# Head by head first quarter, loads of two query blocks into the ring, and a state-space loop mixed with top-k

## The chip, the cores and the metric

The program runs on one core of a Trainium2 chip. A core has a matrix engine (PE, with its weight loads as PEld), a vector engine (DVE), a scalar engine (ACT), a general engine (POOL, which here only issues gathers once the start is over), a queue engine (SP, which issues the plain loads) and 16 DMA engines that all loads share. The metric is the device time of one execution in microseconds, a median over runs.

## What is computed

A decoder trunk of two layers over 256 positions of width 1024, in float32. Layer 0 mixes with a state-space layer (64 groups of 16 channels, 64 complex states each, then a gated projection, GLU), layer 1 with dilated attention. Each is followed by a PEER channel mixer, which is where most of the time goes. Cut to what matters:

```python
def s5_mixer(h, ...):                  # per group: s[t] = a * s[t-1] + B u[t]; y = Re(C s) + d * h
    ...
    y = jax.nn.gelu(y).astype(h.dtype)
    z = y @ w_glu
    val, gate = jnp.split(z, 2, axis=-1)
    return val * jax.nn.sigmoid(gate)

def peer_ffn(h, w_q, sub_keys, u_tab, v_tab):
    q = (h @ w_q).reshape(bsz, seq, PEER_HEADS, 2, PEER_HALF)       # 8 heads, 2 halves of 128
    s = jnp.einsum('blhpe,hpne->blhpn', q, sub_keys)                # 128 keys a half
    s_top, i_top = lax.top_k(s, PEER_TOPK)                          # 16 of 128, each half
    cand = s_top[..., 0, :, None] + s_top[..., 1, None, :]          # 256 sums a head
    best, pos = lax.top_k(cand, PEER_TOPK)                          # 16 experts a head
    gate = jax.nn.softmax(best, axis=-1)
    # per token: sum over 8 * 16 experts of gate * gelu(u_e . h) * v_e
```

Every token reads 128 rows of u and v (8 KB an expert), chosen by its own top-k.

## The kernel before

The 256 positions are two chunks of 128, so there are four **phases**: PEER of layer 0 for chunk 0 (phase 0) and chunk 1, then of layer 1 for both. A phase is 128 gathers ("slots"). One gather (L1160, POOL) is an indirect DMA of 128 rows, 1.05 MB, into one of eight ring places in `ringmem`. DVE multiplies the u part with the spread activations and sums it (L1189, "a dot product"), ACT applies gelu and the gate (L773, L777, L782), PE multiplies the v part into PSUM (L419). Slots go in **pairs** (64 a phase). Gather s waits until PE has used pair (s - 8) // 2 (`v_pe`), so POOL runs at most eight slots ahead.

While phase p runs, the engines also do the next dense stage: in phase 0 it is layer 0 for chunk 1. Every engine has one instruction stream, written by hand, and `g.at(phase, n)` puts in the slots of the first n pairs before what follows. So `g.at` points set the whole order: in phase 0 the state-space loop starts at pair 14 with a step every 4 pairs (`S5_AT, S5_K = 14, 4`), the GLU projections stand at 46 to 49, the norm at 51, the next PEER scores from 54.

Eight heads go in four **quarters** of two heads. A quarter is 32 of the 128 slots. For each: PE projects queries from one 2.1 MB block of w_q (L492, 32 matmuls, which the trace shows as 64 records), ACT copies them (`copy_q`, L966), PE scores them against the keys (`score`, L588), DVE does the top-k in four parts (`best_of_halves`, `sum_pairs`, `best_of_sums`, `find_experts`, L1426 to L1488), and ACT lays the indices out as gather rows (`gate_quarter`, L850 to L859), which counts up `idx_ready`. Only then can the gathers of that quarter go. In phase 0 the first quarter runs before any gather. DVE then has the parts of quarters 1 to 3 at points 1 to 12 (`other_quarters(0, 1)`), each behind one more pair, and the state-space loop follows. A step k of that loop is PE's input product (`s5_bu`, L529), DVE's rotation (`s5_rotate`, L1293 to L1301) and scan (`s5_scan`, L1311 to L1319), PE's output product (`s5_y`, L548) and ACT's gelu. There are eight steps (KT = 8).

All quarters of the top-k share one scratch place (`qs` and gT). Weights go through two places, `wt[:, 0]` and `wt[:, 1]`, in one numbered sequence of items (`weights`): item n is loaded when item n - 2 is used. SP issues them in the order of its stream, so one that waits holds up all behind it.

## Time and profile before

| | |
|---|---|
| median of 3 runs | 1776.49 us (1765.98 to 1777.57) |
| profiled execution | 1767.9 us, span 1766.1 us, granted TensorE clock 0.858 |
| busy, share of span | PE 72%, DVE 63%, ACT 38%, POOL 35% |
| DMA | 685.81 MB, mean 388 GB/s; gathers 536.90 MB |
| chain that ended last | PE 34%, DMA 32%, DVE 18%, ACT 8%, issue 5%, POOL 3% |

The page cuts the span into 40 slices of 44 us; the rows of the section below come from it and from answers about single stretches. Times in a timeline are from the start of the span. "Idle before <- X" says what ended an engine's wait. The share of DMA is the mean busy share of its 16 engines; values a little over 1 are full.

### The profile page before, as it was taken

To read this page: it belongs to the slowest core of one execution; us is meant where nothing else is said; L and a number is where in the kernel's file an instruction comes from. 1 tells how busy PE (TensorE), PEld (TensorE's weight loads), DVE (VectorE), ACT (ScalarE), POOL (GpSimd) and SP (SyncE) were. 2 spreads that over 40 slices of the span, in tenths; PEclk is the share of its full clock that TensorE was granted. 3 is DMA by queue.
4 is the path that set the end of the run, shared out by engine and by line. 5 is a ranking of instruction groups with operands and counts; after the bars stand their busy time and mean duration, and the time that the engine had idled before them with its cause. 6 is when DMAs were issued, how large, how long until landed. Compare 5 with 4: busy or idle time off the path is not lost.

```text
span 1766.1 us, 17527 instructions
## 1 busy us (share of the span) xinstructions
PE 1279.0 (72%) x5714; PEld 537.8 (30%) x5714; DVE 1118.9 (63%) x2512; ACT 675.6 (38%) x2012; POOL 616.9 (35%) x557
## 2 busy tenths in 40 slices
PE   3884455576976988997778599799886965555554
PEld 2471011122721333333345133443352720000000
DVE  8859888973569656435346975553553577666554
ACT  7634522222243338217323432741572243233222
POOL 4213243442243224324322322332432254444341
PEclk9998667789987988999898799899998987676777
DMA  8059999999998999999999899999999989999996
GB/s 330 7 232 380 380 420 397 410 413 423 423 421 338 425 424 421 423 425 421 423 424 416 342 416 424 421 357 426 422 372 424 404 356 416 416 417 410 421 421 291
DMA packets 86636, 685.81 MB, mean 388 GB/s; under 512 B 9872, under 2 KB 10256, under 8 KB 12176
## 3 DMA queue, kind: packets, MB, share of 16 engines
q0 software_dynamic: 73728, 536.90, 74.2%
q1 hardware_dynamic: 12816, 147.79, 20.0%
q8 instruction: 45, 0.74, 0.2%
q14 instruction: 47, 0.39, 0.1%
HBM read 683.60 MB, written 1.05 MB: 388 GB/s over the span
## 4 chain that ended last, share of the span: by engine, by line
PE 34%; DMA 32%; DVE 18%; ACT 8%; issue 5%; POOL 3%; SPq 0%; POOLq 0%; ACTq 0%; DVEq 0%
DMA ringmem<-experts,lay 22%; PE ps L480 12%; PE ps L419 11%; DMA wt<-w_qkv 7%; PE ps L492 6%; DVE ringmem L1189 5%; POOL ringmem L1160 3%; DMA wt<-w_o 2%; ACT lay L850 2%; ACT S L782 2%; PE ps L432 1%; PE ps L661 1%; ACT L777 1%; PE ps L686 1%; DMA wt<-w_glu 1%
## 5 line engine op out<-in xcount | busy, mean ns | idle before, releaser
L1160 POOL DMA_INDIRECT ringmem<-experts,lay x512 | 585.4, 1143 | 1070.9 <-PE ps L419 939.6
L419 PE MATMUL ps<-ringmem,S 128*32 128x512 f32 x2048 | 619.6, 765 | 389.0 <-ACT S L782 387.0
L1189 DVE CUSTOM_DVE_ANT_0 ringmem<-ringmem,Hrep 128x1024 f32<-128x1024 f32 x384 | 460.7, 1223 | 256.1 <-DMA ringmem<-experts,lay 251.3
L419 PEld LDWEIGHTS ps<-ringmem,S 128*32 128x32 f32 x2048 | 113.8, 126 | 800.2 <-ACT S L782 547.4
L777 ACT ACTIVATE gelus<-dots 128x2 f32<-128x2 f32 x256 | 51.6, 202 | 593.5 <-DVE dots L1189 592.5
L480 PE MATMUL ps<-wt,hT 128*128 128x512 f32 x576 | 256.2, 598 | 13.8 <-DMA wt<-w_qkv 13.8
L1189 DVE CUSTOM_DVE_ANT_0 ringmem<-ringmem,area 128x1024 f32<-128x1024 f32 x128 | 155.7, 1224 | 119.4 <-DMA ringmem<-experts,lay 118.4
L480 PEld LDWEIGHTS ps<-wt,hT 128*128 128x128 f32 x576 | 106.5, 190 | 164.0 <-issue 158.7
L773 ACT ACTIVATE S<-con,lay 128x32 f32<-128x32 f32 x512 | 134.6, 311 | 50.7 <-PE ps L419 50.0
L782 ACT ACTIVATE S<-S,gelus 128x32 f32<-128x32 f32 x512 | 136.7, 314 | 24.8 <-ACT gelus L777 1.5
L492 PEld LDWEIGHTS ps<-hT,wt 128*128 128x128 f32 x1024 | 117.4, 194 | 10.6 <-issue 10.3
L492 PE MATMUL ps<-hT,wt 128*128 128x128 f32 x1024 | 120.1, 279 | 0.0
L480 PE MATMUL ps<-wt,gT 128*128 128x512 f32 x128 | 62.3, 643 | 12.4 <-DMA wt<-w_o 10.5
L777 ACT ACT_TABLE_LOAD x55 | 70.6, 1283 | 1.0
L850 ACT COPY lay<-sel 32x16 f32<-32x16 f32 x256 | 51.5, 201 | 38.4 <-DVE sel L1488 35.6
L1509 DVE TENSOR_TENSOR area<-ps,con 128x512 f32<-128x512 f32 x24 | 16.6, 691 | 75.3 <-PE ps L480 63.1
L1024 ACT COPY area<-ps 128x512 f32<-128x512 f32 x12 | 7.0, 586 | 141.4 <-PE ps L480 141.4
L1524 DVE CUSTOM_DVE_ANT_0 area<-ps,area 128x384 f32<-128x384 f32 (+1 forms) x32 | 24.2, 757 | 46.1 <-PE ps L661 46.1
L1426 DVE MAX8 qs<-ps 128x8 f32<-128x128 f32 x64 | 14.2, 283 | 53.9 <-PE ps L515 42.7
L661 PE MATMUL ps<-area 64*128 64x128 f32 x288 | 43.2, 295 | 0.0
L1189 DVE DVE_READ_ACCUMULATOR2_ANT dots<- 128x1 f32 x512 | 41.7, 81 | 0.0
L998 ACT ACT_TABLE_LOAD x32 | 41.1, 1283 | 0.6
(201 smaller groups left out, 1163.4 us busy)
## 6 DMA issues: line engine op xcount, KB each, us to landing
wt<-w_qkv SPq DMA_DIRECT2D x36, 2048.0 KB, 11.6
wt<-w_q SPq DMA_DIRECT2D x16, 2048.0 KB, 11.4
wt<-w_glu SPq DMA_DIRECT2D x5, 2048.0 KB, 12.6
ringmem<-experts,lay POOLq DMA_INDIRECT x512, 12.5
wt<-w_o SPq DMA_DIRECT2D x4, 2048.0 KB, 14.5
ringmem<-w_glu SPq DMA_DIRECT2D x3, 2048.0 KB, 21.4
gain<-gains SPq DMA_DIRECT2D x9, 512.0 KB, 14.4
area<-keys SPq DMA_DIRECT2D x4, 1024.0 KB, 9.6
```

The costliest lines, as they stand in the source:

```text
L419: last = pe.matmul(ps[TG * t:TG * (t + 1), half, :], S[:, u % 2, i, :], ring[:, (2 * u + i) % RING, D + half * 512:D + (half + 1) * 512], ...
L480: last = pe.matmul(ps[:, bank, :], act[:, k, :], wt[:, n % 2, k, :], start=(k == 0), stop=(k == KT - 1))
L492: last = pe.matmul(ps[:, bank, m * P:(m + 1) * P], wt[:, n % 2, k, m * P:(m + 1) * P], hT[:, k, :], start=(k == 0 and m == 0), stop=(k == ...
L661: last = pe.matmul(ps[:, 2 + at // 512, at % 512:at % 512 + P], QT[rows, gr, h // 2, :], kt, start=True, stop=True, skip_group_check=True)
L773: last = act.activation(S[:, u % 2, i, :], own, ACT.Copy, scale=lay[:, phase % NC, 1, j - 1 + i, n:n + 1])
L777: act.activation(gelus[:, u % 2, :], dots[:, u % 2, :], ACT.Gelu_apprx_tanh).then_inc(gelu_ready, 1)
L782: last = act.activation(S[:, u % 2, i, :], S[:, u % 2, i, :], ACT.Copy, scale=gelus[:, u % 2, i:i + 1])
L850: last = act.copy(lay[TG * r:TG * (r + 1), ph % NC, :, j, n:n + QPQ], sel[TG * j:TG * (j + 1), :, QPQ * r:QPQ * (r + 1)])
L998: act.activation(SS[u % 2][:, 0:n], SS[u % 2][:, 0:n], ACT.Exp, bias=nmx[:, u:u + 1], scale=DH ** -0.5, accum_out=den[:, u:u + 1]).then_in ...
L1160: pool.indirect_dma_start(ring[:, s % RING, :], None, experts[phase // NC], bass.IndirectOffsetOnAxis(ap=rows[:, phase % NC, j, n:n + 1], ...
L1189: last = v.tensor_tensor_reduce(ring[:, i, 0:D], ring[:, i, 0:D], hrep(phase, j), 1.0, 0.0, ALU.mult, ALU.add, dots[:, b, second:second + 1])
L1524: v.tensor_tensor_reduce(SS[u % 2][:, 0:n], banks(2, 4)[:, at:at + n], mask[:, 0:n], 1.0, NEG, ALU.add, ALU.max, mx[:, u:u + 1]).then_inc( ...
```

## The change

Phase 0 and the dense stage beside it are put in another order; arithmetic and bytes stay the same.

- **First quarter head by head.** PE projects head 0 alone (parts 0 and 1), scores it, and DVE and ACT take its top-k and rows to the end; then head 1. `idx_ready` counts one more, and POOL waits for the second head at slot 16.
- **w_q blocks of quarters 2 and 3 in the ring.** They are loaded into ring places 4 to 7 as soon as the GLU weights there are used, and projected before quarter 1. Gathers 4 and 6 wait for these projections (`wq_used`). Quarters 2, 3 and 1 are all scored before DVE begins quarter 1.
- **Own places for the top-k of quarters 2 and 3,** in `wt[:, 1]`, to which ACT copies their scores. So `wt[:, 1]` holds no weights until their rows are done: only the first GLU block of chunk 1 is loaded early.
- **State-space loop mixed with top-k.** Quarter 1's parts stand at points 4 to 7, those of quarters 2 and 3 at 9 to 34, and the loop's steps at 10 to 46, first step four pairs earlier, the end at 46 as before.

The diff, cut to its core (the top-k functions take their tiles from `top_k_at` and run over the heads they are given, else as before):

```diff
--- before.py
+++ after.py
...
+WT0 = 2
...
+    if layer == 0:
+        return i - WQ0 if c == 0 else WT0 + i
+    return WT0 + ITEMS0 + ITEMS1 * c + i
...
+        wq_ring = [view(ringmem, 4096 * i, KT, BLOCK) for i in (2, 3)]
...
+        late = wt[:, 1].rearrange("p k n -> p (k n)")
+        late_scores = [view(late, 1024 + 512 * i, QHP, NKEYS) for i in range(2)]
+        places = top_k_places(qs, gflat)
+        late_places = top_k_places(late[:, 2048:2560], late)
+
+        def top_k_at(ph, i):
+
+            return late_places if ph == 0 and i >= 2 else places
+
...
+        def event(ph, i, heads=(0, QH)):
+
+            if ph == 0 and i == 0:
+                return heads[1]
+            return QUARTERS * ph + i + 2
+
+        FIRST = [(0, 0, (h, h + 1)) for h in range(QH)]
+        BANKS0 = (5, 6, 7, 4)
+        PARTS0_AT = (4, 5, 6, 7, 9, 13, 17, 21, 25, 27, 30, 34)
...
+        S5_AT = 10, 14, 19, 23, 28, 32, 37, 41, 46
...
-        S5_AT, S5_K = 14, 4
...
-            weights(0, 0, 6, 8)
             next_gain(2, 0)
-            sp.wait_ge(idx_ready, QUARTERS)
-            weights(0, 1, 0, 2)
+            sp.wait_ge(glu_used, 4)
+            for i in range(2):
+                sp.dma_start(wq_ring[i].rearrange("p k n -> p (k n)"), w_q[0, 2 + i]).then_inc(wq_in[i], 16)
+            weights(0, 1, 0, 1)
             next_gain(3, 1)
-            weights(0, 1, 2, 6)
+            sp.wait_ge(idx_ready, event(0, QUARTERS - 1))
+            weights(0, 1, 1, 6)
             load_keys(1, glu_done, 2)
...
-                project_turned(item(0, 0, WQ0), 4, e)
+                project_turned(item(0, 0, WQ0), 4, e, parts=(0, 1), done=first_q)
                 pe.wait_ge(keys_in, 16)
-                score(0)
+                score(1, 4, 0, (0, 1))
                 pe.wait_ge(con_in, 16)
                 spread_first()
-                for i in range(1, QUARTERS + 1):
-                    if i < QUARTERS:
-                        project_turned(item(0, 0, WQ0 + i), 4 + i)
-                    if i >= 2:
-                        score(i - 1)
+                project_turned(item(0, 0, WQ0), BANKS0[0], parts=(2, 3))
+                score(2, BANKS0[0], 0, (2, 3))
+                pe.wait_ge(best_ready, 1)
+                for i in (2, 3):
+                    pe.wait_ge(wq_in[i - 2], 16)
+                    project_turned(None, BANKS0[i], done=wq_used, w=wq_ring[i - 2])
+                g.at(0, 1)
+                score(3, BANKS0[2], 2)
+                score(4, BANKS0[3], 3)
+                g.at(0, 2)
+                project_turned(item(0, 0, WQ0 + 1), BANKS0[1])
+                g.at(0, 3)
+                score(5, BANKS0[1], 1)
 
...
-                    g.at(gphase, S5_AT)
+                    g.at(gphase, S5_AT[0])
                     pe.wait_ge(hT_ready, e + 1)
-                    pe.wait_ge(idx_ready, QUARTERS)
+                    pe.wait_ge(best_ready, event(0, 1))
+                    pe.wait_ge(score_copied, 1)
...
-                copy_q(0)
+                def copy_q(i, bank, parts=slice(0, QHP)):
+                    act.copy(qT[:, i % 2, parts].rearrange("p k t -> p (k t)"),
+                             ps[:, bank, P * parts.start:P * parts.stop]).then_inc(q_copied, 1)
+
+                act.wait_ge(first_q, 1)
+                copy_q(0, 4, slice(0, 2))
                 act.wait_ge(z0_ready, KT)
                 spread_h()
-                gate_quarter(0, 0)
-                for i in range(1, QUARTERS):
-                    copy_q(i)
+                gate_quarter(*FIRST[0])
+                act.wait_ge(w_used, item(0, 0, WQ0) + 1)
+                copy_q(0, BANKS0[0], slice(2, 4))
+                gate_quarter(*FIRST[1])
+                act.wait_ge(wq_used, 1)
+                act.wait_ge(score_done, 2)
+                copy_q(2, BANKS0[2])
+                g.at(0, 1)
+                act.wait_ge(wq_used, 2)
+                copy_q(3, BANKS0[3])
+                g.at(0, 3)
+                act.wait_ge(w_used, item(0, 0, WQ0 + 1) + 1)
+                act.wait_ge(score_done, 4)
+                copy_q(1, BANKS0[1])
+                for i in range(2):
+                    last = act.copy(late_scores[i].rearrange("p a n -> p (a n)"), ps[:, BANKS0[2 + i], :])
+                last.then_inc(score_copied, 1)
+                g.at(0, PARTS0_AT[0])
+                copy_turn(hT, turned, norm_event(0, 1, 0) + 1, hT_ready)
+                g.at(0, PARTS0_AT[3])
+                gate_quarter(0, 1)
 
...
-                copy_turn(hT, turned, e + 1, hT_ready)
...
+                for n in range(S5_AT[0] + 1, S5_AT[KT] + 1):
+                    g.at(gphase, n)
+                    if n in PARTS0_AT[7::4]:
+                        gate_quarter(0, PARTS0_AT.index(n) // TOPK_PARTS + 1)
+                    if n in S5_AT:
+                        k = S5_AT.index(n) - 1
+                        if k + 1 < KT:
+                            spread_step(k + 1)
+                        gelu_y(c, k)
                 g.at(gphase, GLU_AT + 4)
...
+                if phase == 0 and at == QSTEPS // QH:
+                    pool.wait_ge(idx_ready, event(0, 0))
+                if s in (4, 6):
+                    pool.wait_ge(wq_used, s // 2 - 1)
...
-                top_k(None, 0, 0, 0)
+                top_k(None, 0, *FIRST[0])
 
             def layer0(gphase, c):
-                for k in range(KT):
-                    if k == 0:
-                        g.at(gphase, S5_AT + 1)
+                for n in range(PARTS0_AT[0], S5_AT[KT] + 1):
+                    g.at(gphase, n)
+                    if n in PARTS0_AT:
+                        i, part = divmod(PARTS0_AT.index(n), TOPK_PARTS)
+                        top_k_part(0, i + 1, part)
+                    if n == S5_AT[0]:
                         v.wait_ge(z0_ready, KT)
                         v.tensor_tensor(z0re, z0re, mag, ALU.mult)
                         link(v.tensor_tensor(z0im, z0im, mag, ALU.mult))
+                    if n == S5_AT[0] + 2:
+                        s5_scan(c, 0)
+                    if n - 1 in S5_AT[1:KT]:
+                        s5_scan(c, S5_AT.index(n - 1))
+                    if n == S5_AT[0] + 1:
                         s5_rotate(c, 0)
-                    g.at(gphase, S5_AT + S5_K * k + 1)
-                    s5_scan(c, k)
-                    g.at(gphase, S5_AT + S5_K * (k + 1))
-                    if k + 1 < KT:
-                        s5_rotate(c, k + 1)
+                    if n in S5_AT[1:KT]:
+                        s5_rotate(c, S5_AT.index(n))
...
+                w = top_k_at(ph, i)
+                if ph == 0 and i >= 2:
+                    sc = late_scores[i - 2]
+                    v.wait_ge(score_copied, 1)
+                else:
+                    bank = 4 + i if ph else 4 if heads == (0, 1) else BANKS0[i]
+                    sc = ps[:, bank, :].rearrange("p (a n) -> p a n", a=QHP)
...
-            other_quarters(0, 1)
+            top_k(None, 0, *FIRST[1])
```

PE between the first PEER projection and the state-space loop, before. L492 is a projection, L588 a score group, L432 the spread of the activations, L458 the transpose for chunk 1, L419 the slots (4 matmuls a pair).

```order
L470 MATMUL ps<-con,H 128x128 x8
L492 MATMUL ps<-hT,wt 128x128 x32
L588 MATMUL ps<-area 128x128 x4
L432 MATMUL ps<-H,con 128x512 x8
L492 MATMUL ps<-hT,wt 128x128 x64
L588 MATMUL ps<-area 128x128 x4
L492 MATMUL ps<-hT,wt 128x128 x32
L588 MATMUL ps<-area 128x128 x8
L458 MATMUL ps<-con,H 128x128 x8
L419 MATMUL ps<-ringmem,S 32x512 x56
```

The same place on PE in the change, where L523 is a projection, L619 a score group, L461 the spread and L448 the slots.

```order
L523 MATMUL ps<-hT,wt 128x128 x16
L619 MATMUL ps<-area 128x128 x2
L461 MATMUL ps<-H,con 128x512 x8
L523 MATMUL ps<-hT,wt 128x128 x16
L619 MATMUL ps<-area 128x128 x2
L523 MATMUL ps<-hT,ringmem 128x128 x64
L448 MATMUL ps<-ringmem,S 32x512 x4
L619 MATMUL ps<-area 128x128 x8
L448 MATMUL ps<-ringmem,S 32x512 x4
L523 MATMUL ps<-hT,wt 128x128 x32
L448 MATMUL ps<-ringmem,S 32x512 x4
L619 MATMUL ps<-area 128x128 x4
```

The first projection and score group are halved, quarters 2 and 3 go first, and three pairs now stand ahead of the scores of quarter 1.

DVE between the scan of step 2 and the rotation of step 3 of the loop, before. L1317 to L1319 end the scan, L1189 is a dot product and the read of its sum (three pairs stand here, one dot product is shown), L1293 begins the rotation.

```order
L1317 TENSOR_TENSOR area<-area 128x512
L1318 SCALAR_TENSOR_TENSOR area<-area 128x512
L1319 TENSOR_TENSOR area<-area 128x512
L1189 ISA ringmem,dots<-ringmem,Hrep 128x1024
L1189 ISA dots 128x1
L1293 TENSOR_TENSOR area<-area,ps 128x512
```

The same place in the change: one pair, then the last part of a top-k in `wt`, then two pairs and the rotation (L1361).

```order
L1387 TENSOR_TENSOR area<-area 128x512
L1257 ISA ringmem,dots<-ringmem,Hrep 128x1024
L1257 ISA dots 128x1
L1558 TENSOR_SCALAR wt<-wt 128x32
L1559 TENSOR_SCALAR wt<-wt 128x32
L1561 CAST wt<-wt 128x64
L1566 TENSOR_TENSOR wt<-wt,con 128x1024
L1570 TENSOR_TENSOR wt<-wt 128x512 x2
L1573 TENSOR_REDUCE wt<-wt 128x64
L1576 SCALAR_TENSOR_TENSOR sel<-wt 128x32
L1581 TENSOR_TENSOR sel<-wt 128x32
L1361 TENSOR_TENSOR area<-area,ps 128x512
```

A part of top-k has moved into the space between two steps of the loop, on the same engine.

## Rows read from the trace of the kernel before

**Rows 1.** The page: the span, and what the DMA engines moved in 40 slices.

```profile
span 1766.1 us, 17527 instructions
...
GB/s 330 7 232 380 380 420 397 410 413 423 423 421 338 425 424 421 423 425 421 423 424 416 342 416 424 421 357 426 422 372 424 404 356 416 416 417 410 421 421 291
```

**Rows 2.** Stretches: us, busy PE, PEld, DVE, ACT, POOL, granted clock, DMA share, GB/s.

```profile
94.50:122.70 28.20, 27.43 (x196) 24.10 (x196) 15.17 (x64) 8.22 (x20) 0.00 (x0) 0.93 0.38 141
...
134.90:211.00 76.10, 34.04 (x118) 8.14 (x116) 74.45 (x239) 34.98 (x125) 26.56 (x24) 0.73 0.92 372
211.00:246.00 35.00, 17.34 (x113) 4.93 (x113) 26.03 (x47) 10.48 (x40) 13.19 (x12) 0.70 1.01 423
246.00:383.40 137.40, 81.20 (x525) 22.51 (x526) 122.07 (x198) 38.67 (x152) 57.38 (x52) 0.72 1.00 408
```

**Rows 3.** Timeline from first PEER projection to first gather: start, us, engine, line.

```profile
94.51 9.34 PE L492 MATMUL ps<-hT,wt 128*128 128x128 f32 x64
...
103.88 0.59 ACT L966 COPY area<-ps 128x512 f32<-128x512 f32 x1 [8.47 <-PE ps L492]
...
105.84 0.89 DVE L1426 MAX8 qs<-ps 128x8 f32<-128x128 f32 x4 [11.19 <-PE ps L588]
...
110.72 14.56 PE L492 MATMUL ps<-hT,wt 128*128 128x128 f32 x128
...
121.15 0.19 DVE L1488 TENSOR_TENSOR sel<-qs 128x32 f32<-128x32 f32 x1
...
121.37 0.84 ACT L850 COPY lay<-sel 32x16 f32<-32x16 f32 x4 [5.68 <-DVE sel L1488]
...
122.73 1.12 POOL L1160 DMA_INDIRECT ringmem<-experts,lay  x1 [39.13 <-ACT lay L854]
```

**Rows 4.** Timeline of DVE over one quarter's top-k with four pairs between.

```profile
159.50 0.89 DVE L1426 MAX8 qs<-ps 128x8 f32<-128x128 f32 x4
...
162.68 1.23 DVE L1189 CUSTOM_DVE_ANT_0 ringmem<-ringmem,Hrep 128x1024 f32<-128x1024 f32 x1
...
164.97 0.87 DVE L1435 MAX8 qs<-gT 128x8 f32<-128x128 f32 x4
...
184.08 0.89 DVE L1426 MAX8 qs<-ps 128x8 f32<-128x128 f32 x4
```

**Rows 5.** Timeline of one step of the state-space loop, and a pair's way to its gather.

```profile
260.06 0.69 DVE L1293 TENSOR_TENSOR area<-area,ps 128x512 f32<-128x512 f32 x1 [1.01 <-issue]
...
264.49 1.23 DVE L1189 CUSTOM_DVE_ANT_0 ringmem<-ringmem,Hrep 128x1024 f32<-128x1024 f32 x1
...
266.79 1.22 DVE L1311 TENSOR_TENSOR_SCAN area<-qs,area 128x512 f32<-128x512 f32 x1
...
267.79 3.63 PE L419 MATMUL ps<-ringmem,S 128*32 128x512 f32 x8 [5.12 <-ACT S L782]
...
271.70 0.94 POOL L1160 DMA_INDIRECT ringmem<-experts,lay  x1 [6.57 <-PE ps L419]
271.72 1.24 DVE L1189 CUSTOM_DVE_ANT_0 ringmem<-ringmem,Hrep 128x1024 f32<-128x1024 f32 x1
```

**Rows 6.** Waits of DVE, 134.9 to 383.4 us: total, times, longest.

```profile
DVE ringmem L1189 <- DMA ringmem<-experts,lay: 10.4, 11, 2.1
DVE area L1293 <- issue: 8.5, 6, 2.1
DVE area L1293 <- PE ps L529: 3.6, 1, 3.6
```

**Rows 7.** A stretch in the columns of rows 2.

```profile
95.00:100.00 5.00, 5.00 (x32) 5.00 (x32) 0.00 (x0) 0.41 (x2) 0.00 (x0) 0.64 0.19 77
```

**Rows 8.** Gathers to 389 us and their way to landing; DVE at dot product 91.

```profile
L1160 POOL DMA_INDIRECT ringmem<-experts,lay x100: 932/938/1974, 122.7 to 388.3; - x100
...
DMA to landing us min/median/max: 5.6/10.6/21.8
...
382.13 1.26 DVE L1189 CUSTOM_DVE_ANT_0 ringmem<-ringmem,Hrep 128x1024 f32<-128x1024 f32 x1 [1.14 <-DMA ringmem<-experts,lay]
```

More of the change, by code:

```diff
@@ L21 @@
+from collections import namedtuple
 from contextlib import ExitStack
@@ L227, in build @@
         glu_used = sem("glu_used")
+        wq_in = [sem(f"wq_in{i}") for i in range(2)]
+        wq_used = sem("wq_used")
         w_used = sem("w_used")
@@ L263, in build @@
         q_copied = sem("q_copied")
+        first_q = sem("first_q")
         score_done = sem("score_done")
@@ L1448, in best_of_sums @@
-            def best_of_sums(ph, c, i):
-                cand2 = S2.rearrange("p (h two) n -> p h (two n)", two=2)
-                for h in range(QH):
-                    last = v.max(best[:, h, 0:8], cand[:, h, :])
+                hs = slice(*heads)
+                ms = slice(2 * heads[0], 2 * heads[1])
+                pairs = w.stop.rearrange("p (h two) k -> p h two k", two=2)
+                v.tensor_copy(w.itopf[:, ms], w.itop[:, ms])
+                shape = [P, heads[1] - heads[0], TOPK, TOPK]
@@ new lines, in sum_pairs, with best_of_sums @@
+                link(v.tensor_tensor(w.cand.rearrange("p h (i j) -> p h i j", j=TOPK)[:, hs],
+                                     spread(pairs[:, hs, 0, :], 3, shape),
+                                     spread(pairs[:, hs, 1, :], 2, shape), ALU.add))
+            def best_of_sums(ph, i, heads):
+                w = top_k_at(ph, i)
+                cand2 = w.S2.rearrange("p (h two) n -> p h (two n)", two=2)
+                hs = slice(*heads)
+                for h in range(*heads):
+                    last = v.max(w.best[:, h, 0:8], w.cand[:, h, :])
```

219 lines of the change are left out of this document (107 added, 112 removed).

## The prediction

> **What bounds the kernel now.** I read the slices of the page first: of the 40 slices of 44 us, the second and third move 7 and 232 GB/s, the fourth and fifth 380, and nearly all behind them close to 420 [rows 1]. The 512 gathers of 1.05 MB are 537 of 686 MB, so past the first gather time is bytes over rate plus DMA idle. The table by stretch [rows 2] shows where DMA is idle: from 94.5 us (first PEER projection) to the first gather it is busy 0.38 of 28.2 us, 17.5 us idle, and from 134.9 to 211.0 us it is busy 0.92 of 76.1 us, 6.1 us idle. Those 23.6 us are all that an earlier start and a better mix can win in phase 0. The same table says who holds DMA back in the second stretch: DVE is busy 74.45 of 76.10 us (top-k of quarters 1 to 3). In the state-space loop it is busy 122.07 of 137.40 us, with DMA just full at 408 GB/s. So in phase 0 **two** limits lie close together: DMA, 2.48 us a gather at 423 GB/s (2.57 at the loop's 408), and DVE. After phase 0 nothing is touched: the reworked top-k helpers issue the same instructions on the same number of elements there.
>
> **DVE's prices, start to start.** A dot product takes 1.15 us, a pair 2.30 (162.68 to 164.97). One quarter's top-k and four pairs take 184.08 - 159.50 = 24.58 us, so the top-k is 24.58 - 9.20 = 15.4 us; its first part is 162.68 - 159.50 = 3.2 [rows 4]. A state-space step is a rotation of 264.49 - 260.06 = 4.43 and a scan of 271.72 - 266.79 = 4.93, together 9.36 us [rows 5].
>
> **First gather.** The projection of head 0 is 32 of the 64 records of 9.34 us; the stretch 95 to 100 us holds 32 records, so it ends near 99.7, 4.2 us before [rows 3, 7]. Copy and scores halve: -0.7. Of the 15.4 us of top-k some ten instructions are as small as the last one (0.19 us, some 0.14 start to start) and keep their time, 1.4 us; the rest halves: 1.4 + 7.0 = 8.4, so -7.0. First gather: 122.73 - 11.9 = 110.8 us [rows 3]. This is the gain the change makes. The two w_q blocks (4.2 MB, 10 us at 423 GB/s) and a gain load now run from 95 to 106, where DMA was idle.
>
> **What it costs behind.** ACT copies head 1's queries only after head 0's index rows: those ended 4.4 us after 121.3, so now 109.4 + 4.4 = 113.8, and PE gets them at 114.2, scores done at 115.0. PE has by then sat 5 us. It then has quarters 2 and 3 (14.6 us at full clock, the 128 records of 14.56 [rows 3]), pair 0, two score groups, pair 1, quarter 1 (7.3), pair 2, and the score group of quarter 1, which is the one DVE needs next. With 2.6 us for a pair (between 3.63 at half clock [rows 5] and half of it) and 1.1 for a score group: 115.0 + 14.6 + 2.0 (a start at half clock, as 9.34 - 7.28 of the first projection) + 2.6 + 2.2 + 2.6 + 7.3 + 2.6 + 1.1 = 150.0 us. Gathers 4 to 7 also wait for the ring slots that hold w_q, to about 124 and 131.6. DVE has head 1 (8.4 us from 115) and pairs 0 to 3 done by 140 and then waits 10 us. So **quarter 1's top-k starts at 150 with four pairs done, where before it started at 134.9 with one**: three pairs are worth 6.9 us, the delay is 15.1, and DVE is 8 us behind. Bounds: 148 with every projection at full clock; 157 with quarter 1's projection wholly at half.
>
> Two edits I cost at nothing: the copies of the late scores (two of the kind of 0.59 [rows 3]) run on ACT while DVE waits for quarter 1, and ACT is busy 34.98 of 76.10 us [rows 2]; and the late top-k reads and writes SBUF places instead of PSUM and gT, on as many elements. If a late part cost 10% more, DVE would lose 3 us.
>
> **The mixed stretch.** From pair 9 to pair 34 DVE now has 25 pairs (57.5), two top-k (30.8) and six steps (56.2): 144.5 us, 5.8 a pair, before any wait, where DMA needs 4.95 to 5.14. Both regimes that are alternated load DVE, so DVE stays the bound. Its waits: before, 8.5 + 3.6 us over seven of the eight rotations on PE, up to 2.1 each, 3.6 for the first [rows 6]. Now rotations 1 and 4 stand behind a top-k part and wait for nothing; 2 and 5 pay 2.1, and 3 waits for pairs that ACT holds up behind a gate quarter (3.4 us of copies), say 3.0. With the first's 3.6 that is 10.8, and I add 2.1 for small ones: 12.9 us to point 34 (5 to 17). Pair 33 ends at 150.0 + 30 x 2.30 + 46.2 + 56.2 + 0.2 + 12.9 less the last part of 5.0 behind it = 329.5. From a pair's last dot product to its gather takes 271.70 - 266.87 = 4.8 us [rows 5], the second of two 1.2 more, and landing at least 5.6 [rows 8]: gather 75 lands at 341.1. Before, gather 91 had landed at 382.1 and 16 gathers at 2.57 are 41.1: gather 75 at 341.0 [rows 8]. Equal, but before had read both first w_glu blocks of chunk 1 by then and the new order has one of them left: 2.1 MB, 5.0 us. A further 1.8 us of DMA idle I put beside the gate of the last quarter at point 34. Gather 91 then lands at 341.1 + 5.0 + 41.1 + 1.8 = 389.0, **6.9 us later than before** at the same bytes. The same from DVE alone: 150.0 + 42 x 2.30 + 46.2 + 74.9 + 0.2 + 19.2 (the 12.9, 4.2 for rotation 6 behind the last gate, 2.1 for rotation 7) = 387.1 against 383.3 now, +3.8; the later of the two counts. Behind it everything is DMA-bound in both. The sum: 12 us won at the first gather, given back between 110 and 340 with 7 us on top. The profiled execution (span 1766.1, 1767.9 with what lies around it) becomes 1774.8; the median of the three runs is 1776.49, so I forecast 1783.4 in its terms. This case's own range: waits 5 to 17 and start 148 to 157 give -4 to +18.
>
> The Trainium skill, Perfetto Trace Analysis, section Optimization Strategy, says performance may improve by interleaving regimes whose most-contended engine differs. That would favour this change; rows 2 show DVE as the fullest engine in both regimes, so its condition isn't met here.
>
> **Rivals.** (a) *The early start survives.* If quarter 1 is scored by 140 and the ring of eight (four pairs, 20 us of gathers) bridges DVE's lag, DMA never starves: gain 12 us, at most 23.6 less the 6 us between the w_q loads and the first gather, 17.6: 1759 to 1765. For it: DVE idles 10.4 us on DMA before, which it could use. Against it: 5.8 us a pair over 25 pairs is a lag of 17 to 21 us without waits. (b) *PE's clock.* PE sat idle before the first projection and the granted clock was 0.64 in 95 to 100 us [rows 7]; the new order puts 5 us of idle before quarters 2 and 3 and small gaps before quarter 1. If all three run at 1.2 instead of 2.4 GHz, quarter 1's scores come up to 3 x 7.3 - 2 = 20 us later; with quarter 1 and half of the others 11 to 13: the kernel ends 18 to 25 us later, 1795 to 1808. It decides from about 10 us of extra PE time. The Trainium skill, TensorE: Matmul & The Clock Gate, Part 1, says the throttled clock is the default and activity lifts it; the trace agrees (0.64 there with 9.34 us for 64 records, then 14.56 us for 128 [rows 3]). (c) *Nothing shows.* DVE's lag and the won start cancel within 4 us, 1773 to 1781.
>
> **Chances.** Forecast 0.50; (a) 0.18, of which 0.11 beyond 1%; (b) 0.20, nearly all beyond 1%; (c) 0.12. One per cent is 17.8 us, about what a measurement of this kernel can tell from no change. Faster 0.12, same 0.66, slower 0.22 ((b) and the top of the forecast). The range 1762 to 1804 leaves out 0.1 of (a) below and less than 0.1 of (b) above.
>
> **What would show it.** First gather at 110 to 112 us; gathers 4 and 6 waiting on PE to about 124 and 131; DVE idle some 10 us before quarter 1's first MAX8, which starts near 150; DVE over 0.93 busy and DMA under 400 GB/s between 165 and 330 us; rotation waits near zero for the second and fifth; gather 99 issued about 7 us later than 388.3. It is wrong if quarter 1 starts before 145, or if DMA moves 420 GB/s through the mixed stretch: then (a).

## The result, and the profile after

| | before | the change |
|---|---|---|
| median | 1773.01 us (1764.5 to 1777.57, 10 runs) | 1784.22 us (1775.89 to 1795.96, 10 runs) |
| ratio, 95% interval | | 1.0073 (1.0047 to 1.010) |
| profiled execution, span | 1766.1 us | 1782.1 us |
| first gather; gather 99, counted from 0 | 122.73; 388.3 us | 112.03; 399.6 us |

The kernel became 0.73% slower, by more than its measurement is uncertain; the forecast of 1783.4 us lies 0.8 us from the median. The page of the change, the rows that answer to [rows 1]:

```profile
span 1782.1 us, 17568 instructions
...
GB/s 327 12 345 394 362 318 358 346 401 426 422 422 348 427 422 421 423 425 421 424 421 422 352 416 424 413 352 425 422 363 425 415 321 407 414 418 412 420 422 289
```

The third slice of 44.6 us moves 345 GB/s where it moved 232, but the fifth to eighth move 362, 318, 358 and 346 where they moved 380, 420, 397 and 410. Behind them the two are alike. The same by stretch, in the columns of [rows 2]:

```profile
94.50:122.70 28.20, 25.68 (x135) 21.33 (x135) 15.96 (x70) 11.11 (x35) 3.93 (x4) 0.75 0.77 310
134.90:211.00 76.10, 45.93 (x263) 18.36 (x261) 63.52 (x171) 25.38 (x93) 30.77 (x29) 0.82 0.93 370
211.00:246.00 35.00, 20.32 (x96) 5.37 (x96) 30.69 (x60) 8.32 (x33) 12.71 (x12) 0.66 0.98 395
246.00:383.40 137.40, 72.55 (x416) 19.43 (x416) 117.06 (x235) 44.21 (x165) 54.20 (x45) 0.71 0.89 347
```

DMA is busy 0.77 of the first stretch (it was 0.38) and 0.89 of the last (it was 1.00). DVE does 117 us of work in the last stretch where it did 122, though it now has the last part of quarter 2's top-k and all of quarter 3's there beside the loop: it waits instead. Its waits from 134.9 to 383.4 us, as in [rows 6] (L1361 begins a rotation, L1257 is a dot product, L1505 a top-k's first MAX8):

```profile
DVE area L1361 <- issue: 23.3, 6, 7.0
DVE ringmem L1257 <- DMA ringmem<-experts,lay: 5.5, 5, 1.5
DVE qs L1505 <- PE ps L619: 4.4, 1, 4.4
```

Before, DVE waited 10.4 us for gathers and 12.1 us at rotations; now 5.5 and 23.3. It has changed from an engine that is at times ahead of DMA to one that seldom is. The rotation waits, which the profile marks "issue", are for a product on PE; a timeline below shows it.

The gathers, counted from 0 in the timelines of POOL, show where the won start is lost. Gather 0 goes 10.7 us earlier than before, gather 32 goes 12.7 us earlier (205.3 for 218.0) and gather 44 still 12.8 us (237.4 for 250.2). Gather 64 goes 1.4 us later than before and gather 75 already 11.0 us later (337.7 for 326.7). So the won start is still whole at gather 44, and all of it and 11 us more go between 240 and 340 us, in the mixed loop.

### The profile page after: what moved, and what is told of

The parts are those of the page before. It is cut to its first block, busy times and chain, and to the rows that moved or that the text cites. A ratio compares the mean times of both kernels' runs of the same rounds, so it can differ in the third digit from the quotient of the medians.

```text
span 1782.1 us, 17568 instructions
## 1 busy us (share of the span) xinstructions
PE 1293.5 (73%) x5714; PEld 543.7 (31%) x5714; DVE 1119.5 (63%) x2526; ACT 682.3 (38%) x2033; POOL 621.5 (35%) x557
## 4 chain that ended last, share of the span: by engine, by line
PE 32%; DMA 28%; DVE 9%; ACT 7%; issue 4%; POOL 2%; POOLq 0%; ACTq 0%; SPq 0%; DVEq 0%
DMA ringmem<-experts,lay 17%; PE ps L509 12%; PE ps L448 10%; DMA wt<-w_qkv 8%; PE ps L523 5%; DVE ringmem L1257 4%; POOL ringmem L1228 2%; DMA wt<-w_o 2%; ACT lay L895 2%; ACT S L824 1%; PE ps L726 1%; PE ps L701 1%; ACT L819 1%; PE ps L461 1%; PE ps L712 1%
## 5 line engine op out<-in xcount | busy, mean ns | idle before, releaser
L448 PE MATMUL ps<-ringmem,S 128*32 128x512 f32 x2048 | 625.9, 765 | 395.6 <-ACT S L824 387.2
L1257 DVE CUSTOM_DVE_ANT_0 ringmem<-ringmem,Hrep 128x1024 f32<-128x1024 f32 x384 | 460.0, 1223 | 245.8 <-DMA ringmem<-experts,lay 232.6
L448 PEld LDWEIGHTS ps<-ringmem,S 128*32 128x32 f32 x2048 | 114.2, 127 | 804.7 <-ACT S L824 545.3
L819 ACT ACTIVATE gelus<-dots 128x2 f32<-128x2 f32 x256 | 52.0, 203 | 585.5 <-DVE dots L1257 574.2
L509 PE MATMUL ps<-wt,hT 128*128 128x512 f32 x576 | 257.9, 601 | 14.2 <-DMA wt<-w_qkv 14.1
L1257 DVE CUSTOM_DVE_ANT_0 ringmem<-ringmem,area 128x1024 f32<-128x1024 f32 x128 | 155.5, 1225 | 116.6 <-DMA ringmem<-experts,lay 116.0
L523 PEld LDWEIGHTS ps<-hT,wt 128*128 128x128 f32 x896 | 105.4, 198 | 12.1 <-issue 11.9
L523 PE MATMUL ps<-hT,wt 128*128 128x128 f32 x896 | 108.3, 283 | 0.0
L895 ACT COPY lay<-sel 32x16 f32<-32x16 f32 (+1 forms) x272 | 55.0, 202 | 37.6 <-DVE sel L1581 33.2
L1602 DVE TENSOR_TENSOR area<-ps,con 128x512 f32<-128x512 f32 x24 | 16.6, 690 | 79.7 <-PE ps L509 65.0
L1505 DVE MAX8 qs<-ps 128x8 f32<-128x128 f32 x56 | 12.5, 284 | 58.4 <-PE ps L546 42.5
L1257 DVE DVE_READ_ACCUMULATOR2_ANT dots<- 128x1 f32 x512 | 42.1, 82 | 0.0
## 6 DMA issues: line engine op xcount, KB each, us to landing
wt<-w_q SPq DMA_DIRECT2D x14, 2048.0 KB, 12.1
```

Source lines behind the costliest of these rows:

```text
L448: last = pe.matmul(ps[TG * t:TG * (t + 1), half, :], S[:, u % 2, i, :], ring[:, (2 * u + i) % RING, D + half * 512:D + (half + 1) * 512], ...
L509: last = pe.matmul(ps[:, bank, :], act[:, k, :], wt[:, n % 2, k, :], start=(k == 0), stop=(k == KT - 1))
L523: last = pe.matmul(ps[:, bank, m * P:(m + 1) * P], w[:, k, m * P:(m + 1) * P], hT[:, k, :], start=(k == 0 and m == parts[0]), stop=(k == K ...
L819: act.activation(gelus[:, u % 2, :], dots[:, u % 2, :], ACT.Gelu_apprx_tanh).then_inc(gelu_ready, 1)
L895: last = act.copy(lay[TG * r:TG * (r + 1), ph % NC, :, j, n:n + width], sel[TG * j:TG * (j + 1), :, at + width * r:at + width * (r + 1)])
L1257: last = v.tensor_tensor_reduce(ring[:, i, 0:D], ring[:, i, 0:D], hrep(phase, j), 1.0, 0.0, ALU.mult, ALU.add, dots[:, b, second:second + 1])
```

## The experiments

All ran beside the kernel before, on the same chip in each batch. Medians differ a little between batches, so the ratio to before is what compares. Two kernels of different batches compare only by these ratios, and a difference of two ratios is uncertain by some 0.3 to 0.4%. Here they are together; gathers are counted from 0, and the last two columns are from each profiled execution.

| kernel | ratio (95% interval) | gather 16, 64, 99 at us | waits at rotations, us |
|---|---|---|---|
| before | 1 | 167.4, 302.0, 388.3 | 12.1 |
| the change | 1.0073 (1.0047 to 1.010) | 158.2, 303.4, 399.6 | 23.3 |
| e1_heads_alone | 1.0109 (1.0077 to 1.0141) | 187.7, 322.7, 409.1 | 9.2 |
| e6_heads_gain_first | 1.0049 (1.0029 to 1.0069) | 175.7, 309.6, 396.1 | 9.1 |
| e2_unmixed | 1.0032 (1.0008 to 1.0055) | 157.5, 305.3, 393.4 | 19.7 |
| e3_q1_first | 1.0069 (1.0044 to 1.0094) | 160.0, 303.4, 401.1 | 17.4 |
| e5_rows_later | 1.0031 (1.0011 to 1.0051) | 158.6, 298.7, 395.1 | 13.8 |
| e8_product_early | 0.996 (0.9938 to 0.9983) | 157.9, 291.7, 384.9 | 2.7 |
| e7_early_and_rows | 0.9963 (0.9942 to 0.9985) | 157.9, 292.2, 383.9 | 2.7 |
| e9_before_early | 0.996 (0.9937 to 0.9982) | 167.7, 300.9, 385.1 | 4.0 |
| e12_load_mixed | 1.0077 (1.0058 to 1.0096) | 158.7, 305.9, 402.8 | 17.5 |
| e13_load_late | 1.0078 (1.0055 to 1.0102) | 158.5, 304.1, 399.5 | 25.3 |
| e10_unmixed_early | 1.0025 (1.0 to 1.0049) | 158.6, 304.2, 392.2 | 18.1 |
| e11_q1_unmixed_early | 0.9992 (0.9973 to 1.0011) | 159.6, 298.9, 383.8 | 10.5 |

**One part alone: head by head.** The first quarter is split as in the change, all else stays as before.

```diff
-        PARTS0_AT = (4, 5, 6, 7, 9, 13, 17, 21, 25, 27, 30, 34)
-        S5_AT = 10, 14, 19, 23, 28, 32, 37, 41, 46
+        PARTS0_AT = (1, 2, 3, 4, 5, 6, 7, 8, 9, 10, 11, 12)
+        S5_AT = 14, 18, 22, 26, 30, 34, 38, 42, 46
...
+            weights(0, 0, 6, 8)
             next_gain(2, 0)
-            for i in range(2):
-                sp.dma_start(wq_ring[i].rearrange("p k n -> p (k n)"), w_q[0, 2 + i]).then_inc(wq_in[i], 16)
```

> Only the first quarter head by head; w_q blocks, places, quarters 1 to 3 at points 1 to 12 and the loop at 14 to 46 as before. Mine (the early start is real, the rest gives it back): first gather at 112, quarter 1's top-k at about 128 where before began at 134.9, so DVE is 6 to 7 us ahead and the kernel ends 4 to 10 us earlier than before (ratio 0.995 to 0.998). Rival (an early start is worth nothing in any order, because DMA catches up anyway): ratio 1.000 within 0.002. Rival (head by head itself costs, through two half top-k): slower than before.

The first gather came at 111.9 us as expected, and the kernel was 1.1% slower. The timeline of that run, SP and DVE (start, us, engine and line):

```profile
109.96 14.96 SPq L389 DMA_DIRECT2D wt<-w_q  x2
124.97 0.43 SPq L393 DMA_DIRECT2D gain<-gains  x1
...
140.04 1.28 DVE L1273 SCALAR_TENSOR_TENSOR H<-X,stat,gain 128x1024 f32<-128x1024 f32 x1 [29.42 <-issue]
```

The gain of the norm of chunk 1 is 0.5 MB. SP has it behind the two w_q loads, and the second of these waits for a free place in `wt`, so the gain was issued only at 125 us. That is 14.3 us of the wait. The other 15.1 us lie behind the issue, with DMA full (share 1.01, 423 GB/s from 125 to 140 us): the gain shared it with w_q and eight early gathers. DVE stood 29.4 us before that norm, with the top-k of head 1 behind it; in the kernel before, the same norm waited 6.0 us. The change moves this load ahead (issued at 93 us), which my list of its edits had put down among what fills idle DMA. So this run tests a worse kernel than the part alone, and the next one mends it.

```diff
-            weights(0, 0, 6, 8)
             next_gain(2, 0)
+            weights(0, 0, 6, 8)
```

> The run with head by head alone (ratio 1.011, vector engine stalled 29.4 us before its norm of the second chunk), with one edit: the gain load is issued ahead of the two w_q loads of quarters 2 and 3. Theory (the small gain load, queued behind 4.2 MB and eight gathers, cost that run its won start): the 29.4 us wait is gone, the second head's top-k starts near 113 to 115 us, quarter 1's near 128 to 132, and the ratio to the kernel before is 0.996 to 1.000. Rival (what is late is the whole w_q stream, which now shares the DMA engines with the eight early gathers, so that projections and scores of quarters 2 and 3 stay late): the wait moves to the scores of quarter 1 or 2, and the ratio is 1.002 to 1.008.

The 29.4 us are gone and the ratio is 1.0049, 0.6% better than without this edit, but still slower than before: the rival's range. The rest of the w_q stream is late, as its PE rows show (L521 is a projection, and the two waits are for weights):

```profile
126.50 7.41 PE L521 MATMUL ps<-hT,wt 128*128 128x128 f32 x64 [0.63 <-DMA wt<-w_q]
133.75 1.06 PE L617 MATMUL ps<-area 128*128 128x128 f32 x8
137.66 7.41 PE L521 MATMUL ps<-hT,wt 128*128 128x128 f32 x64 [2.85 <-DMA wt<-w_q]
```

PE takes the slots of the first pair only behind these (at 151.5 us), so gathers 8 and up wait until 153.6 us where they went at 144.8 before. An early first gather is worth nothing if the ring of eight then stands still. The rival gave the eight gathers as the reason, through shared DMA engines. The rows speak for another: SP issued these two loads at 114.1 and about 126.2 us, where before it issued them at 103.9 and about 118.5, since each waits for a place in `wt` that a projection still holds; and DMA was busy only 0.70 from 127 to 153 us. The change loads both blocks into the ring from 93.4 us and has pair 0 ahead of quarter 1's projection, and its gather 8 goes at 135.2 us. No run separates these two.

**Mixed or not.** The change with its top-k in one piece, the loop behind it.

```diff
-        PARTS0_AT = (4, 5, 6, 7, 9, 13, 17, 21, 25, 27, 30, 34)
-        S5_AT = 10, 14, 19, 23, 28, 32, 37, 41, 46
+        PARTS0_AT = (4, 5, 6, 7, 8, 9, 10, 11, 12, 13, 14, 15)
+        S5_AT = 16, 19, 23, 27, 31, 34, 38, 42, 46
```

> The change with its top-k parts in a row at points 4 to 15 and the loop at 16 to 46. Mine (DVE is the bound whatever the mix, only waits for PE differ): rotations 0 to 7 wait 2 to 3 us each, near 20 in all instead of 23.3, gather 99 within 4 us of the change's 399.7, time within 5 us of the change. Rival (mixing top-k into the loop is what costs): back to before or better, 8 to 12 us faster than the change.

0.4% faster than the change, gather 99 at 393.4 us (399.6). That is between my 5 us and the rival's 8 to 12. The mixed order costs some 7 us as it stands, though the two intervals overlap a little. Rotations wait nearly as long (19.7 us), and it is still slower than before. The loop has 30 pairs here and 36 in the change, so its steps also stand closer together.

**Quarter 1 first.** Here the late start of quarter 1 is taken away: PE projects and scores quarter 1 ahead of quarters 2 and 3.

```diff
-                for i in (2, 3):
-                    pe.wait_ge(wq_in[i - 2], 16)
-                    project_turned(None, BANKS0[i], done=wq_used, w=wq_ring[i - 2])
-                g.at(0, 1)
-                score(3, BANKS0[2], 2)
...
+                project_turned(item(0, 0, WQ0 + 1), BANKS0[1])
+                pe.wait_ge(wq_in[0], 16)
+                project_turned(None, BANKS0[2], done=wq_used, w=wq_ring[0])
+                score(3, BANKS0[1], 1)
...
+        PARTS0_AT = (2, 3, 4, 5, 9, 13, 17, 21, 25, 27, 30, 34)
```

> The change with quarter 1 projected and scored before quarters 2 and 3, its parts at points 2 to 5. Mine (DVE's 15 us later start on quarter 1 is the largest loss): quarter 1 starts at 134 to 136 instead of 148.6 with two pairs done instead of four, DVE is 8 to 10 us ahead of the change, gathers 4 to 7 go 7 us later; 5 to 10 us faster than the change, near before. Rival (the mixed stretch alone sets the end, its start does not matter): within 3 us of the change.

Quarter 1's top-k began at 133.9 us instead of 148.6, and nothing came of it: ratio 1.0069, and gather 64 goes at 303.4 us in both. The two are level much earlier, at gather 28 (190.7 and 190.1 us). The waits of DVE in this run, from 134.9 to 383.4 us:

```profile
DVE area L1360 <- issue: 17.4, 7, 6.6
DVE ringmem L1256 <- DMA ringmem<-experts,lay: 11.9, 9, 2.3
```

DVE waited 11.9 us for gathers (5.5 in the change), nearly all of it before the first rotation, which came at 186.7 us and in the change at 186.2. DMA was busy 0.97 from 150 to 211 us, against 0.90. So DVE's lead was spent on waiting for gathers, and part of that is the edit's own: it makes gathers 4 and 8 go 5.2 and 5.5 us later. This speaks against the part of my working that let the late quarter 1 carry through to the end: two starts 14.7 us apart led to the same place 50 us later.

**The waits at rotations, first edit: rows later.** ACT's 16 row copies of a gate quarter stand two pairs behind its exponential instead of right behind it.

```diff
-                        gate_quarter(0, PARTS0_AT.index(n) // TOPK_PARTS + 1)
+                        gate_exps(0, PARTS0_AT.index(n) // TOPK_PARTS + 1)
+                    if n - 2 in PARTS0_AT[7::4]:
+                        gate_rows(0, PARTS0_AT.index(n - 2) // TOPK_PARTS + 1)
```

> The change with ACT's exponential of quarters 2 and 3 where it was (points 21 and 34) and its 16 row copies two pairs later (23 and 36). Mine (rotations 3 and 6 wait for pairs held up behind these copies): rotation 3 waits about 4 instead of 7.0 us, rotation 6 about 2.5 instead of 4.3, 3 to 5 us faster than the change. Rival (the long waits come from PE's clock or from the landing of gathers): both waits unchanged, same time.

The waits of rotations 3 and 6 fell from 7.0 and 4.3 us to 3.6 and 2.0, gather 99 went 4.5 us earlier, and the ratio to before fell by 0.4%, some 7 us, where I expected 3 to 5. The timeline of the change shows why rotation 3 waited so long (L895 is the row copies, L819 the gelu, L448 the slots, L560 the input product of the loop's step):

```profile
253.33 3.42 ACT L895 COPY lay<-sel 32x16 f32<-32x16 f32 x16 [2.62 <-DVE sel L1581]
256.78 0.22 ACT L904 CAST lay<-lay 128x32 uint32<-128x32 f32 x1
256.91 0.53 ACT L815 ACTIVATE S<-con,lay 128x32 f32<-128x32 f32 x2
257.46 1.28 ACT L819 ACT_TABLE_LOAD   x1
258.75 0.21 ACT L819 ACTIVATE gelus<-dots 128x2 f32<-128x2 f32 x1
...
259.64 3.63 PE L448 MATMUL ps<-ringmem,S 128*32 128x512 f32 x8 [7.17 <-ACT S L824]
...
263.20 1.24 PE L560 MATMUL ps<-hT,area 32*128 32x128 f32 x16
...
264.89 0.69 DVE L1361 TENSOR_TENSOR area<-area,ps 128x512 f32<-128x512 f32 x1 [7.00 <-issue]
...
263.55 0.94 POOL L1228 DMA_INDIRECT ringmem<-experts,lay  x1 [8.29 <-PE ps L448]
```

The rotation needs the input product. PE has that product behind the slots of the last pair but one, these wait for ACT's gates, and ACT is copying rows and then loads the gelu table again (1.28 us; it had loaded another for the exponential at 249.19 us). DVE, which had been ready since 257.9 us, waits for a product whose own inputs were there long before.

**The second edit: product early.** If so, it is enough to put the product elsewhere on PE, with DVE and ACT left as they are.

```diff
                 for k in range(KT):
-                    g.at(gphase, S5_AT[k + 1] - 1)
                     if k + 1 < KT:
+                        g.at(gphase, S5_AT[k] + 2)
                         s5_bu(c, k + 1)
+                    g.at(gphase, S5_AT[k + 1] - 1)
```

> The change, with one edit on the matrix engine: the input product of the next step stands two pairs behind the last rotation instead of one pair ahead of its own. Theory (the rotation waits of 23.3 us in six of eight are what the mixed loop loses on the vector engine): they fall under 5 us together, the DMA share from 246 to 383 us rises from 0.89 to 0.95 or more, gather 99 goes out 8 to 15 us earlier than 399.7, and the kernel is 8 to 15 us faster than the change, a ratio to before of 0.998 to 1.003. Rival (the vector engine's work alone, not its waits, sets the pace there, or the waits turn up at the next pair's sums): within 3 us of the change, ratio 1.005 to 1.009.

0.996 against 1.0073: 1.1%, or 20 us, from moving 16 matmul records per step of the loop on PE. I had expected 8 to 15 us and a ratio of 0.998 at best. Its waits of DVE from 150 to 384 us, and the stretches of the loop:

```profile
DVE ringmem L1258 <- DMA ringmem<-experts,lay: 9.8, 8, 1.4
DVE ringmem L1258 <- issue: 2.8, 1, 2.8
DVE area L1362 <- issue: 2.7, 1, 2.7
```

```profile
211.00:246.00 35.00, 20.25 (x102) 5.27 (x104) 34.45 (x67) 10.46 (x38) 16.07 (x12) 0.70 0.97 393
246.00:383.40 137.40, 77.71 (x479) 22.71 (x475) 121.89 (x240) 46.28 (x181) 59.55 (x50) 0.75 0.96 391
```

20.6 us of rotation waits are gone, DMA moves 391 instead of 347 GB/s, and gather 99 goes 14.7 us earlier (expected 8 to 15). The waits for gathers rise to 9.8 us (from 0.4 over the same stretch): DVE is now ahead of DMA at times. The rotation that waited 7.0 us waits for nothing, with the same row copies and the same table load beside it. This kernel is faster than the one before, by 0.4% (0.2 to 0.6).

Both edits together:

> The early input product and the later row copies together. The two act on the same waits (the later rows shortened rotations 3 and 6 by 3.5 and 2.3 us). Theory that the waits are one resource: 0 to 3 us better than the early product alone. If their gains add, 7 us better than it, a ratio of 0.994 to 0.999.

0.9963: no better. The two edits took the same waits.

The same edit in the kernel before:

> The kernel before, with the same edit: the input product two pairs behind the last rotation. Its rotations wait 12.1 us in seven, but DMA is full beside them (share 1.00, 408 GB/s from 246 to 383 us). Theory (a wait costs only where DMA is not full): the waits go and the time stays within 3 us, ratio 0.998 to 1.001. Rival (every wait of the vector engine is on the path): 10 to 12 us faster, ratio 0.993 to 0.994.

Also 0.996, faster than I expected (0.998 to 1.001). My reason for expecting nothing was that the DMA share was 1.00 beside those waits. The loop's stretch in this run:

```profile
246.00:383.40 137.40, 83.20 (x544) 23.10 (x544) 123.26 (x201) 39.16 (x153) 68.60 (x54) 0.74 1.01 419
```

It moves 419 GB/s where it moved 408 at a share of 1.00 [rows 2]. A share of 1.00 was thus not the full rate, and 11 GB/s over 137.4 us are 1.5 MB, 3.6 us: gather 99 went 3.2 us earlier. The rest of the 7 us lies behind gather 99 and is not explained by these rows.

**Is it DVE's time or PE's order?** The early product takes waits off DVE and also moves work on PE. To test DVE's time alone, eight maximum instructions that nothing needs were put on DVE, in the mixed stretch and, as a control, behind the loop.

```diff
+        LOAD_AT = (11, 14, 17, 20, 23, 26, 29, 32)
...
+                    if n in LOAD_AT:
+                        v.max(spare[:, LOAD_AT.index(n)], X[:, 1, :])
```

> The change, with eight extra maximum instructions of the vector engine over 1024 elements (into a place that nothing reads) at points 11, 14, 17, 20, 23, 26, 29 and 32, in the mixed stretch. By the 0.87 us of one over 256 elements times two, and 1.2 us of other instructions over 1024, they are 1.1 us each, near 9 us in all. Theory (the vector engine's time, work and waits alike, is on the path in the mixed stretch): the kernel is 6 to 9 us slower than the change, gather 99 near 407, ratio to before 1.010 to 1.012. Rival (the early input product won 20 us by letting the matrix engine's slot products and so the gathers go earlier, not by the vector engine's waits): the extra work fills the rotation waits or lags behind DMA, within 3 us of the change, 1.005 to 1.009.

```diff
+                for n in range(4):
+                    g.at(gphase, GLU_AT + 1 + n)
+                    for j in range(2):
+                        v.max(spare[:, 2 * n + j], X[:, 1, :])
```

> The same eight instructions, two each at points 47 to 50, behind the state-space loop, where the vector engine waits for gathers. Both theories: no change, within 2 us of the change (ratio 1.006 to 1.008). It is slower by 4 us or more only if the vector engine bounds that stretch too.

The ratios are 1.0077 and 1.0078, both as the change within their intervals. The groups of the extra instructions, early and late, and the rotation waits with the early ones:

```profile
L1462 DVE MAX8 spare<-X 128x8 f32<-128x1024 f32 x8 | 9.8, 1222 | 0.0
```

```profile
L1478 DVE MAX8 spare<-X 128x8 f32<-128x1024 f32 x8 | 9.4, 1216 | 0.0
```

```profile
DVE area L1363 <- issue: 17.5, 6, 4.9
```

9.8 us of work were added and the waits fell by 5.8 us, because several of the eight stand right ahead of a rotation, where DVE would have waited. Net 4.0 us; gather 99 goes 3.1 us later with the early load and 0.2 us earlier with the late one. That fits DVE's time counting one for one, once what falls into waits is taken off, but the ratios can't tell 4 us from nothing. My 6 to 9 us missed, and 1.0077 lies in the range of the rival, that the early product wins by letting slots and gathers go earlier and not by DVE's waits. The test was badly placed and decides less than it should. What it does show is that more than half of the added work vanished into the waits, which can't be when DVE's own work alone sets the pace. That the pace is set by the way from a dot product over ACT and PE back to DVE is how I read this together with the two edits on that way (rows later, product early); no run shows it by itself.

**Combinations.** The unmixed order, and the one with quarter 1 first besides, with the product early:

> The unmixed order of the change (top-k at points 4 to 15, the loop at 16 to 46; ratio 1.003, rotation waits of 19.7 us) with the early input product. Theory (unmixing won 7 us and the early product 20 us by different things, the DMA idle around 180 and 260 us, and the waits): 3 to 7 us better than the mixed order with the early product, gather 99 at 378 to 382, ratio 0.992 to 0.995. Rival (both only take the same rotation waits off the path, and DMA is the bound once they are gone): as the mixed order with the early product, gather 99 at 383 to 386, ratio 0.995 to 0.998.

> As the one before, but quarter 1 projected and scored ahead of quarters 2 and 3, so that its top-k starts near 134 us instead of 148, with the top-k at points 2 to 13 and the loop at 14 to 46 as in the kernel before. Theory (once the loop no longer waits, the start won by the head-by-head order and an early quarter 1 reach the end): gather 99 at 375 to 381, 10 us before that of the kernel before, ratio 0.990 to 0.994. Rival (the late start of quarter 1 costs nothing here either, as in the mixed order): within 2 us of the run before it.

1.0025 and 0.9992: neither beats the mixed order with the same edit. The first lies above both ranges that were expected of it. The second is some 6 us faster than the first, where I expected more and the rival at most 2 us. In the first, rotations still wait 18.1 us, of which 10.5 us are these two:

```profile
230.59 0.69 DVE L1364 TENSOR_TENSOR area<-area,ps 128x512 f32<-128x512 f32 x1 [6.38 <-issue]
...
325.32 0.69 DVE L1364 TENSOR_TENSOR area<-area,ps 128x512 f32<-128x512 f32 x1 [4.16 <-issue]
```

The edit moves neither product. The first is that of step 0. The second is that of the rotation at point 34, three pairs behind the one at 31, where two pairs behind the last rotation and one ahead of the next are the same point. The steps of 4 pairs have theirs moved by one pair. One of these, from the timeline:

```profile
279.61 3.63 PE L448 MATMUL ps<-ringmem,S 128*32 128x512 f32 x8 [3.61 <-ACT S L825]
...
281.02 0.20 ACT L820 ACTIVATE gelus<-dots 128x2 f32<-128x2 f32 x1 [1.04 <-DVE dots L1260]
282.12 1.23 DVE L1260 CUSTOM_DVE_ANT_0 ringmem<-ringmem,Hrep 128x1024 f32<-128x1024 f32 x1
283.16 1.03 PE L560 MATMUL ps<-hT,area 32*128 32x128 f32 x16
...
284.92 0.69 DVE L1364 TENSOR_TENSOR area<-area,ps 128x512 f32<-128x512 f32 x1 [1.56 <-issue]
```

Here only pairs stand between scan and rotation, and DVE does one in 2.3 us. The slots of a pair end on PE some 4.6 us behind its last dot product (278.6 to 283.2 us, at half clock), so a product two pairs ahead is still late. In the mixed order a part of top-k stands in that space and covers it. In e9 and late in e11 DVE waits for gathers instead, and the two pairs are enough.

So **in the new order mixing was ahead by 0.6% with the product early** (0.996 against 1.0025) **and behind by 0.4% with it late** (1.0073 against 1.0032): how good it is to mix depends on that placement. That it is the mixing alone isn't shown. The edit does less in the unmixed run, as said, and the old order, unmixed, reaches 0.996 with the early product as well.

Bytes moved between 94.5 and 384 us, each as rate by time, give the account up to gather 99. Before moved 374 GB/s by 289.5 us, 108.3 MB; the change 358, 103.6 MB; the change with the product early 381, 110.3 MB; the kernel before with it 380, 110.0 MB. 4.6 MB less are 11 us at 420 GB/s, close to the 11.3 us by which gather 99 is late; the profiled spans differ by 16.0, and the 4.7 us between are not explained.

```profile
94.50:384.00 289.50, 171.84 (x1058) 71.04 (x1057) 241.38 (x549) 96.89 (x352) 106.56 (x96) 0.75 0.92 374
94.50:384.00 289.50, 176.09 (x1001) 74.43 (x1000) 235.56 (x549) 96.88 (x355) 107.09 (x92) 0.75 0.90 358
94.50:384.00 289.50, 178.26 (x1066) 76.05 (x1065) 245.16 (x565) 100.69 (x376) 117.55 (x99) 0.77 0.94 381
94.50:384.00 289.50, 175.49 (x1067) 73.66 (x1067) 243.50 (x553) 97.81 (x355) 116.51 (x99) 0.76 0.93 380
```

The rows are of before, the change, the change with the product early and before with it, in the columns of [rows 2].

## Why the prediction was right, point by point

The rows of the change that these points read, first from its timeline, then three stretches in the columns of [rows 2]:

```profile
94.20 5.80 PE L523 MATMUL ps<-hT,wt 128*128 128x128 f32 x32
...
112.03 1.11 POOL L1228 DMA_INDIRECT ringmem<-experts,lay  x1 [28.74 <-ACT lay L899]
...
116.19 15.72 PE L523 MATMUL ps<-hT,ringmem 128*128 128x128 f32 x128
...
125.04 0.94 POOL L1228 DMA_INDIRECT ringmem<-experts,lay  x1 [8.16 <-PE ps L523]
...
132.19 0.94 POOL L1228 DMA_INDIRECT ringmem<-experts,lay  x1 [4.36 <-PE ps L523]
...
148.56 0.89 DVE L1505 MAX8 qs<-ps 128x8 f32<-128x128 f32 x4 [4.43 <-PE ps L619]
```

```profile
122.70:134.90 12.20, 11.59 (x95) 9.94 (x94) 7.73 (x17) 7.86 (x31) 4.89 (x4) 1.00 1.00 406
134.90:150.00 15.10, 15.10 (x114) 11.35 (x114) 6.33 (x16) 4.44 (x15) 5.94 (x7) 1.00 1.01 422
165.00:330.00 165.00, 88.59 (x473) 23.11 (x473) 145.88 (x317) 51.08 (x193) 65.46 (x55) 0.74 0.89 347
```

- **First gather** at 110.8 us: it came at 112.03. The projection of head 0 ended at 100.0 us (99.7 forecast), at the low clock (granted 0.66 from 95 to 100 us, as in [rows 7]). Head 0's top-k took 9.3 us from its first MAX8 at 101.35 to 110.65 us, where 8.4 was forecast.
- **Gathers 4 and 6** to about 124 and 131.6 us: 125.04 and 132.19.
- **Quarter 1's top-k** at 150 us: 148.56, behind 15.72 us of ring projections (16.6 forecast). DVE was idle for 13.2 of the 27.3 us before 150, most of it in short waits for gathers, and 4.4 us in one before quarter 1, where I had some 10 in one. The start is as forecast, and yet the conclusion drawn from it was wrong in part, see below.
- **No clock rival.** The granted clock was 1.00 from 122.7 to 150 us (the first two stretches above, third column from the right).
- **DVE waits at rotations:** none at the second and fifth, as forecast; 23.3 us in all against 19.2. The term that was mis-sized most is rotation 3, 7.0 us for 3.0: I counted the 3.4 us of row copies but not the table load behind them (1.28) nor the slots of a pair at half clock (3.63) and the product (1.24) that stand between the late gate and the rotation. Rotation 2 paid 3.9 for 2.1 and rotation 5 paid 3.0 for 2.1; rotation 6 came as costed (4.3 for 4.2).
- **Two edits costed at nothing:** the late top-k was no dearer in `wt` (278 ns a MAX8 against 286 in PSUM), and the two copies of late scores (1.08 us at 146.1) lay ahead of quarter 1's first MAX8. This held.
- **DVE over 0.93 busy from 165 to 330 us:** 0.88 (145.88 of 165.0 us), so this sign failed. DMA was under 400 GB/s there, as forecast.
- **Gather 75** at 335.5 us: 337.7. **Gather 91** was to land at 389.0; DVE began its dot product at 392.7, behind a wait of 1.3 us for it, 10.6 us later than before. **Gather 99** about 7 us late: 11.3.
- **Given back between 110 and 340 us:** not from 110 on. Gather 44 still went 12.8 us ahead at 237 us, and the loss came behind it.
- **Against before:** + 6.9 us in the forecast's terms; the ratio gives + 13 us (8 to 18). The forecast of 1783.4 was close to the median by luck too, because the three runs shown of before had a median 3.5 us above that of ten. The direction held, the place in part, and the size was about half.

What the runs correct is the reasoning. I wrote that DVE is the bound in the mixed stretch, so that a late quarter 1 (three pairs behind, 8 us) would stay in the sum to the end. e3 let it start 14.7 us earlier and gained nothing, with the reserve that it also makes gathers 4 and 8 some 5 us later. e8 changed no DVE instruction and gained 20 us. So much of what the stretch lost lay in DVE's waits for PE, and I had treated these as a small addition (12.9 us on 144.5) rather than as the thing that can be removed. The count came out near since DVE's waits and work both stand in it; that a start reckoned too costly and waits reckoned too cheap made up for each other is in part luck.

The rule of the Trainium skill that I weighed (Perfetto Trace Analysis, Optimization Strategy: interleave regimes whose most-contended engine differs) I set aside because DVE is fullest in both regimes. The trace agrees that mixing lost as the change has it, 0.4% by e2. But with the product early the mixed order is 0.6% ahead of the unmixed one (e8 against e10, with the reserve above), though the fullest engine is the same. So the fullest engine alone did not decide it here: the loop has waits on another engine, and the top-k parts can fill these.

## What to carry to other kernels

Where an in-order engine holds a small product for another engine, put it as early as its inputs allow, not just ahead of its use: behind work that itself waits for the consumer's last results it turns every hiccup of a third engine into a wait. Before moving large pieces to fill idle time, list the short waits of the fullest engine, name what stands ahead of the late instruction on its own queue, and try that one-line move first; here it won as much in the old order as the whole rework and the move together. And an early start is worth only what every later limit lets through, so follow the won time gather by gather to the end of the stretch: here it was whole at gather 44 and gone at gather 64.
